# Griffin block of a two-layer decoder trunk: three input-projection turns change their stationary operand, and one gate-input turn is split around the gates

## The reference, cut to what matters

```python
gate, u = jnp.split(x @ w_in, 2, axis=-1)          # w_in: 2048 x 4096
u = causal_depthwise_conv(u, width=4) + conv_b
r = sigmoid(blockwise(u, gate_a_w) + gate_a_b)     # 8 diagonal blocks of 256 x 256
i = sigmoid(blockwise(u, gate_x_w) + gate_x_b)
a = exp(-8 * r * softplus(-lam))
b = u * i * sqrt(1 - a * a)
h = scan(h_t = a_t * h_{t-1} + b_t)                # over positions
y = (gelu(gate) * h) @ w_out
```

## Time and profile before

| what | us |
|---|---|
| median of 3 runs | 2082.54 |
| lowest and highest | 2081.93 to 2082.73 |
| the profiled execution, its own time | 2081.55 |
| its span, first to last instruction | 2079.8 |
| PE busy in it | 2073.0 |
| DVE busy, ACT busy | 1267.6, 969.2 |

### The profile page before, as it was taken

The page is one execution under the profiler, slowest core; times in us unless marked ns, Lnnn a source line. Parts: engine busy times, 40 slices in busy tenths (PEclk is TensorE's granted clock), DMA queues, the critical chain, the costliest instruction groups (busy, mean ns, idle before and its releaser), DMA issues.

```text
span 2079.8 us, 27469 instructions
## 1 busy us (share of the span) xinstructions
PE 2073.0 (100%) x9438; PEld 1724.6 (83%) x9438; DVE 1267.6 (61%) x1247; ACT 969.2 (47%) x1168; POOL 21.3 (1%) x16
## 2 busy tenths in 40 slices
PE   9999999999999999999999999999999999999999
PEld 8888888888888888888888888888888888888887
DVE  6869666665555565555765565775755555555565
ACT  5595555434444443443654444454444434444442
POOL 0000010000000000000100000010000000000000
PEclk9999999999999999999999999999999999999999
DMA  8667758766766766675566667667767766766763
GB/s 259 195 207 243 257 189 264 246 199 206 237 220 185 241 225 200 214 249 173 186 209 206 210 221 233 194 212 243 229 207 221 241 200 201 240 218 224 240 214 120
DMA packets 245884, 451.34 MB, mean 217 GB/s; under 512 B 18720, under 2 KB 49696, under 8 KB 244768
## 3 DMA queue, kind: packets, MB, share of 16 engines
q1 hardware_dynamic: 239888, 440.93, 66.8%
q10 hardware_dynamic: 5904, 9.18, 1.4%
HBM read 421.72 MB, written 20.97 MB: 213 GB/s over the span
## 4 chain that ended last, share of the span: by engine, by line
PE 99%; DMA 0%; DVE 0%; ACT 0%; SPq 0%; issue 0%
PE ps L495 92%; PE ps L486 3%; PE ps L483 1%; PE ps L620 1%; PE ps L589 0%; PE ps L590 0%; PE ps L588 0%; PE ps L658 0%; PE ps L667 0%; DMA f<-in_x_dram 0%; PE ps L668 0%; PE ps L657 0%; PE ps L545 0%; PE ps L681 0%; PE ps L682 0%; DVE f L1335 0%
## 5 line engine op out<-in xcount | busy, mean ns | idle before, releaser
L1083 DVE TENSOR_TENSOR wl<-wst,wh 128x1024 fp32r<-128x1024 f32 x742 | 886.5, 1219 | 380.0 <-ACT wh L781 377.9
L781 ACT ACTIVATE wh<-wst 128x1024 fp32r<-128x1024 f32 x742 | 770.5, 1059 | 690.5 <-PE ps L495 400.6
L495 PE MATMUL ps<-wh,xin 128*128 128x512 f32 x3072 | 824.5, 390 | 0.0
L495 PE MATMUL ps<-wh,hid 128*128 128x512 f32 x2560 | 695.9, 390 | 0.0
L495 PEld LDWEIGHTS ps<-wh,xin 128*128 128x128 f32 x3072 | 575.7, 188 | 118.9
L495 PEld LDWEIGHTS ps<-wh,hid 128*128 128x128 f32 x2560 | 479.5, 188 | 98.9
L495 PE MATMUL ps<-wl,xin 128*128 128x512 f32 x1536 | 472.9, 389 | 0.0
L495 PE MATMUL ps<-wl,hid 128*128 128x512 f32 x1280 | 404.6, 389 | 0.0
L495 PEld LDWEIGHTS ps<-wl,xin 128*128 128x128 f32 x1536 | 288.3, 188 | 60.0
L495 PEld LDWEIGHTS ps<-wl,hid 128*128 128x128 f32 x1280 | 240.2, 188 | 50.0
L1453 DVE STREAM_TRANSPOSE f<-f 128x1024 f32<-128x1024 f32 x32 | 39.9, 1245 | 178.7 <-DMA f<-sq_by_quad 178.7
(11 more groups left out here) (123 smaller groups left out, 563.8 us busy)
## 6 DMA issues: line engine op xcount, KB each, us to landing
wst<-in_mlp_w_dram SPq DMA_DIRECT2D x512, 512.0 KB, 4.7
wst<-in_moba_w_qkv_dram SPq DMA_DIRECT2D x96, 512.0 KB, 4.6
wst<-in_rg_w_in_dram SPq DMA_DIRECT2D x62, 512.0 KB, 4.5
wst<-in_rg_w_out_dram SPq DMA_DIRECT2D x32, 512.0 KB, 5.6
sq_by_quad<-f SPq DMA_DIRECT2D x128, 128.0 KB, 2.6
f<-sq_by_quad SPq DMA_DIRECT2D x32, 512.0 KB, 4.9
wst<-in_moba_w_out_dram SPq DMA_DIRECT2D x32, 512.0 KB, 5.1
f<-in_x_dram SPq DMA_DIRECT2D x8, 256.0 KB, 6.8
```

The source lines that it names most:

```text
L495: return pe.matmul(dst, src[:, c, part, a * P:(a + 1) * P], (wl if low else wh)[:, s, w], start=(c == 0 and part + low == 0), stop=(c == N ...
L781: act.activation(wh[:, off % SPLITS, :], wst[:, slot, :], ACT.Copy).then_inc(wh_done, 1)
L1083: dve.tensor_tensor(wl[:, off % SPLITS, :], wst[:, off % STAGE, :], wh[:, off % SPLITS, :], ALU.subtract).then_inc(wl_done, 1)
```

## The change

The turns 1, 2 and 3 of u take the form with the tokens stationary, as the gate-input turns do. Their results go the same way: copied out by ACT (`take_in`), stored and read back by SP (`store_in`, `read_in`), transposed by DVE (`turn_in`). Turn 0 of u keeps its form. The order of PE becomes: u turns 1 to 3, gate pieces 0 to 3 (groups 0 and 1), blocks 0 to 3 of gate-input turn 0, gate pieces 4 to 7 (groups 2 and 3), blocks 4 to 7 of gate-input turn 0, then gate-input turns 1 to 3. The weight blocks keep running numbers in the new order: 32 to 35 gates, 36 to 39 gate input, 40 to 43 gates, 44 to 47 gate input. The queues of SP, ACT and DVE are written anew for the stretch, the banks of PSUM for the gate pieces are others, and the lists `work` of the gate-input turns start later, since the splits of the first four blocks lie elsewhere.

The diff without what is only renamed (lines are left out where "..." stands):

```diff
...
+U_TOKEN = 3
+HALF = 4
...
         def gate_bank(gb, o):
-            return ps[:, 2 * (gb % 4) + o // 2, (o % 2) * T:(o % 2 + 1) * T]
+            first = 2 * gb if gb < 4 else 2 + 2 * (gb - 4) % 6
+            return ps[:, first + o // 2, (o % 2) * T:(o % 2 + 1) * T]
+        def turn_of(n):
+            return T_U + 1 + n if n < U_TOKEN else T_G + n - U_TOKEN
...
-            with sp.Fori(1, NG) as t:
-                load_turn(w_in, D + t * COLS, B_U + t * BLOCKS)
-            for gb in range(BLOCKS):
+            def store_in(n):
+                sp.wait_ge(psum_free, turn_of(n) + 1)
+                for i in range(GROUP):
+                    sp.dma_start(to_quad[i], in_out[i * 32:(i + 1) * 32, :, :]).then_inc(in_stored, 16)
+            def read_in(n):
+                sp.wait_ge(in_stored, (n + 1) * (16 * GROUP))
+                if n:
+                    sp.wait_ge(in_turned, n)
+                sp.dma_start(in_quad, by_quad.rearrange("p (i n) -> p i n", i=GROUP)).then_inc(in_back, 16)
+            def move_in(n):
+                return {2: lambda: store_in(n), 3: lambda: read_in(n)}
+            def load_gates(gb, b):
                 w, n0 = (rg_gate_a_w, rg_gate_x_w)[gb % 2], gb // 2 * 2
-                sp.wait_ge(wl_done, B_GATES + gb - (STAGE - 1))
+                sp.wait_ge(wl_done, b - (STAGE - 1))
                 sp.dma_start(wst[:, gb % STAGE, :].rearrange("p (k n) -> p k n", n=LRU_W),
...
+            with sp.Fori(1, NG - 1) as t:
+                load_turn(w_in, D + t * COLS, B_U + t * BLOCKS)
+            load_turn(w_in, D + (NG - 1) * COLS, B_U + (NG - 1) * BLOCKS, move_in(0))
+            first = cols_of(w_in, 0)
+            for unit, b in enumerate((B_GATES, B_G)):
+                also = move_in(1 + unit)
+                for k in range(HALF):
+                    if k in also:
+                        also[k]()
+                    load_gates(unit * HALF + k, b + k)
+                for k in range(HALF):
+                    load_block(first[unit * HALF + k], HALF + k, b + HALF + k)
+            load_turn(w_in, COLS, B_G + BLOCKS)
...
             for t in range(2, NG):
-                load_turn(w_in, t * COLS, B_G + t * BLOCKS, move_g(t - 2))
-            also = {**move_g(2), BLOCKS: input_again, **{BLOCKS + n: f for n, f in move_g(3).items()}}
+                load_turn(w_in, t * COLS, B_G + t * BLOCKS, move_in(U_TOKEN + t - 2))
...
@@ -567,18 +577,23 @@
...
-            turn(xin, 1, B_U + BLOCKS, R_X)
-            pair(xin, B_U + 2 * BLOCKS, R_X, T_U + 2)
-            for gb in range(BLOCKS):
-                if gb in (0, 2):
-                    pe.wait_ge(psum_free, T_G + gb // 2 - 1)
-                elif gb >= 4:
-                    pe.wait_ge(sig_done, gb - 3)
+            token_turn(xin, 4, B_U + BLOCKS, R_X)
+            pe.wait_ge(psum_free, T_U + 1)
+            token_turn(xin, 0, B_U + 2 * BLOCKS, R_X)
+            pe.wait_ge(psum_free, T_U + 2)
+            token_turn(xin, 4, B_U + 3 * BLOCKS, R_X)
+            def gate_piece(gb, b):
+                if gb == 0:
+                    pe.wait_ge(psum_free, T_G - 1)
+                elif gb == 2:
+                    pe.wait_ge(psum_free, T_G)
+                elif gb >= HALF:
+                    pe.wait_ge(sig_done, gb - 2)
                 pe.wait_ge(pair_ready, R_CONV + 2 * (gb // 2) + 2)
-                pe.wait_ge(wl_done, B_GATES + gb + 1)
-                s = gb % SPLITS
+                pe.wait_ge(wl_done, b + 1)
+                s = gb % HALF
...
+            for unit, b in enumerate((B_GATES, B_G)):
+                for k in range(HALF):
+                    gate_piece(unit * HALF + k, b + k)
+                if unit == 0:
+                    pe.wait_ge(sig_done, 1)
+                for k in range(HALF):
+                    kb = unit * HALF + k
+                    pe.wait_ge(wl_done, b + HALF + k + 1)
+                    for c in range(kb * KCH, (kb + 1) * KCH):
+                        for part, low in ((0, 0), (1, 0), (0, 1)):
+                            for a in range(HALVES):
+                                mm = token_step(xin, 0, a, c, part, low, HALF + k)
+                    mm.then_inc(mm_done, 1)
+            for t in range(1, NG):
+                if t == 1:
+                    pe.wait_ge(sig_done, 7)
                 pe.wait_ge(psum_free, T_G + t - 1)
                 token_turn(xin, 4 * (t % 2), B_G + t * BLOCKS, R_X)
...
             def conv_start(g):
-                act.wait_ge(psum_free, T_U + g + 1)
+                if 1 <= g <= U_TOKEN:
+                    act.wait_ge(in_turned, g)
+                else:
+                    act.wait_ge(psum_free, T_U + g + 1)
...
-            for t in range(NG):
-                b = B_U + t * BLOCKS
-                if t:
-                    splits(b, t, AHEAD, AHEAD + 1)
-                    conv_start(t - 1)
-                    splits(b, t, AHEAD + 1, AHEAD + CONV)
-                    if t == 1:
...
-                    conv_hi_part(t - 1)
-                splits(b, t, AHEAD + CONV if t else BLOCKS, LATE)
-                take_hl(t % 2, b, u3[:, t * GROUP:(t + 1) * GROUP, :], hl_copied)
-                splits(b, t, LATE)
-            conv_start(NG - 1)
-            for gb in range(BLOCKS):
-                splits(B_GATES, B_GATES // BLOCKS, AHEAD + gb, AHEAD + gb + 1)
-                act.wait_ge(mm_done, B_GATES + gb + 1)
+            def take_in(n, first, b):
+                act.wait_ge(mm_done, b + BLOCKS)
+                if n:
+                    act.wait_ge(in_turned, n)
...
+                    taken = act.activation(by_part, by_col, ACT.Copy)
+                taken.then_inc(psum_free, 1)
...
+            b, no = B_U + BLOCKS, 1
+            splits(b, no, AHEAD, AHEAD + 1)
+            conv_start(0)
+            splits(b, no, AHEAD + 1, AHEAD + CONV)
+            act.wait_ge(sp_abs, 1)
...
+            conv_hi_part(0)
+            splits(b, no, AHEAD + CONV, LATE)
+            take_in(0, 4, b)
+            splits(b, no, LATE)
+            b, no = B_U + 2 * BLOCKS, 2
+            splits(b, no, AHEAD, AHEAD + 6)
+            conv_start(1)
+            splits(b, no, AHEAD + 6, LATE)
+            take_in(1, 0, b)
+            splits(b, no, LATE)
+            b, no = B_U + 3 * BLOCKS, 3
+            splits(b, no, AHEAD, AHEAD + 1)
+            conv_hi_part(1)
+            splits(b, no, AHEAD + 1, AHEAD + 6)
+            conv_start(2)
+            splits(b, no, AHEAD + 6, LATE)
+            take_in(2, 4, b)
+            splits(b, no, LATE)
+            def gate_values(gb, b):
+                act.wait_ge(mm_done, b + 1)
                 dst, bias = ((r3, C_BA), (i3, C_BX))[gb % 2]
                 for o in range(GROUP):
                     c = gb // 2 * GROUP + o
                     sg = act.activation(dst[:, c, :], gate_bank(gb, o), ACT.Sigmoid, bias=prm[:, bias + c:bias + c + 1])
                 sg.then_inc(sig_done, 1)
-                if gb == 1:
-                    conv_hi_part(NG - 1)
+            for k in range(HALF):
+                splits(B_GATES, B_GATES // BLOCKS, AHEAD + k, AHEAD + k + 1)
+                if k == 1:
+                    conv_hi_part(2)
+                gate_values(k, B_GATES + k)
+            splits(B_GATES, B_GATES // BLOCKS, AHEAD + HALF, AHEAD + HALF + 1)
+            conv_start(3)
+            splits(B_GATES, B_GATES // BLOCKS, AHEAD + HALF + 1)
+            conv_hi_part(3)
+            for k in range(HALF):
+                splits(B_G, B_G // BLOCKS, AHEAD + k, AHEAD + k + 1)
+                gate_values(HALF + k, B_G + k)
             act.wait_ge(sp_ready, 1)
             act.wait_ge(sig_done, 8)
...
-                act.wait_ge(g_turned, g + 1)
+                act.wait_ge(in_turned, U_TOKEN + g + 1)
...
-            work = (((1, decay, 0), (2, decay, 1), (2, decay, 2)),
-                    ((1, decay, 3), (2, root, 0), (0, root, 1), (1, root, 2), (1, root, 3)),
+            work = (((1, decay, 0), (1, decay, 1)),
+                    ((0, decay, 2), (1, decay, 3), (2, root, 0), (0, root, 1), (1, root, 2), (1, root, 3)),
                     ((6, gelu, 0), (0, gelu, 1)),
                     ((1, product_hi, 0), (1, product_hi, 1), (4, gelu, 2), (1, product_hi, 2)))
             for t in range(NG):
                 b, no = B_G + t * BLOCKS, B_G // BLOCKS + t
-                off = AHEAD
+                off = AHEAD if t else AHEAD + HALF
...
-                act.wait_ge(mm_done, b + BLOCKS)
-                if t:
...
+                take_in(U_TOKEN + t, 4 * (t % 2), b)
...
-            for t in range(NG):
-                b = B_U + t * BLOCKS
-                if t:
-                    splits(b, AHEAD, AHEAD + 1)
-                    for k in range(1, CONV):
-                        splits(b, AHEAD + k, AHEAD + k + 1)
-                        conv_step(t - 1, k)
-                    splits(b, AHEAD + CONV, AHEAD + CONV + 1)
-                    conv_lo(t - 1)
```

(70 more changed lines are left out.)

55 lines of the change are left out of this document (19 added, 36 removed).

## The result

In alternating runs on one chip the changed kernel took 2085.04 us (median of 16 runs, 2082.61 to 2089.45), the kernel before 2082.07 (16 runs, 2081.61 to 2082.93). That is 2.97 us longer, a ratio of 1.0018 with an interval of 1.0011 to 1.0025. The forecast was 2081.8: the sign is wrong, and the time lies 0.6 us above the range. It is still within the 0.2% that was called no change. The profiled execution of the changed kernel took 2086.9, 1.9 above its median, with a span of 2085.1. So what its trace shows in excess of the span before (2085.1 - 2079.8 = 5.3) is more than the 2.97 of the medians: it is the fourth longest of the 16 executions.

The account below looks back on a forecast made before the run. PE was taken to bound the kernel. The form's -1.29 us and a new wait of 0.55 at gate piece 6 gave -0.74; from the median 2082.54 that made 2081.8 us, range 2080.8 to 2084.4.

Parts of the forecast that it names:

- What bounds the kernel: Whole program: PE bounds, busy 2073.0 of 2079.8 us; other engines' work counts only if PE then waits.
- The form: u turns 1 to 3 with tokens stationary: 65.30 us instead of 66.59, saving 1.29 us, all on the path.
- The estimate of 0.25: u turns 1 to 3: saving in us by the skill's issue-gap rule, which would make the sum +0.3.
- All this I cost at nothing on the path: u turns: added ACT, DVE, SP and DMA work costs PE nothing, except a new wait at gate piece 6.
- the cover of 8 blocks split ahead: u turns: 8 blocks of 2.72 us split ahead cover PE against block loads late by about 6 us.
- The likeness with the gate-input turns: u turns: PE is covered, as the same moves already stand in the gate-input turns, where PE has no wait.
- The wait at piece 6: Gate piece 6: PE waits for conv_lo(3), due 126.73 against 126.19, so 0.54, say 0.55 us.
- The identity activation between sigmoids: Rival, gates: Identity between sigmoids brings one more table load of 1.28 us; net +0.5, 2083.1; chance 0.03.
- the read-back is late: Rival, u turn 3: one slow DMA, wait 0.55 plus 1 to 3.3 us, net +0.3 to +2.6; chance 0.20.
- The test given for it: Piece 6: a wait over 1.5 us, with DVE waiting on the read near 112, would say the DMAs decide.
- the rival of 8 us: Third turned u: read-back very late, both landings 8.0 us, 6.4 more at piece 6, net +5.7, 2088.2; chance 0.07.
- I take the output projection to be covered: Output projection: no cost from the later recurrence, first need being at 208 with four gate-input turns between.

Follow-up runs that it names:

- two kernels, 0.20: Against the changed kernel: u turns neither stored nor read back, 2082.4 us; all seven read-backs issued one block load later, 2081.41 us.
- the control: Kernel before, with only DVE's addition of output-projection turn 0 one split earlier: 2082.1 us against 2081.87, ratio 1.0001.
- the kernel with group 3 in a row: Changed kernel with DVE's three convolution steps of group 3 before the gated input and splits: 2082.61 us; with the addition one split earlier too: 2080.67.
- the form alone: Changed kernel with gate pieces 6 and 7 on group 2's activations and DVE's output-projection addition one split earlier: 2080.52 us, ratio 0.9994.
- with the addition in its place: Changed kernel with gate pieces 6 and 7 on group 2's activations, DVE's addition not moved: 2082.6 us, ratio 1.0007.
- with the wait at piece 6 present: Changed kernel repeated, 2085.38 us, and the changed kernel with DVE's output-projection addition one split earlier, 2083.62 us.
- with group 3's own data: Changed kernel repeated unaltered on the chip of the next three runs: 2085.38 us, ratio 1.0016 to the kernel before.
- the filled one: Changed kernel with 24 matmuls that nothing reads ahead of PE's wait at gate piece 6: 2085.39 us, ratio 1.0019.

## Why the prediction was wrong, step by step

**What bounds the kernel: right.** Every microsecond gained or lost is one of PE's, and the stretch of u turns, gates and gate-input turns holds all but the last wait.

**The form: right.** 65.30 for three turns was worked out; 65.30 is measured in the changed kernel, and 65.30 to 65.34 in the ones that follow. The switches cost nothing that counts: piece 4 starts at 120.93, 22.42 behind the end of turn 3, where 4 x 2.88 + 10.88 = 22.40. The estimate of 0.25 by "TensorE: Matmul & The Clock Gate" of the Trainium skill, section "Back-to-back issue gap", is not borne out: the trace has 1.29.

**"All this I cost at nothing on the path": the step that failed.** The prediction saw that "the block loads behind them are late by about 6 us" and set the cover of 8 blocks split ahead against it. The cover is PE's: PE indeed waited at no weight block. But the same load is also waited for by ACT's split, and ACT's list is in order. Behind that split stand `conv_start(2)` and `take_in(2)`, on which the convolution of group 3 hangs. The price of a held load had to be carried down ACT's list, not only to PE. What was put at nothing was, in the profiled execution, 2.51 us of lateness that PE waited for at piece 6, and 1.54 of clock behind that wait. The sentence "ACT is in order and has no slack behind the end of that turn", from which the chain was started at 98.03, holds where the load isn't held (two kernels, 0.20) and is wrong in the changed one (1.99 and 2.51).

**The likeness with the gate-input turns misled.** "The same moves already stand in the gate-input turns, where PE has no wait" is true, but in the kernel before no step that PE waits for came late by it there.

**The wait at piece 6: the chain's length was right, its start was not.** From its own start the chain needs 28.75 us against the 28.70 listed, and the table above gives a wait of 0.52 to 0.58 on top of the lateness against 0.54. The term was mis-sized by exactly the lateness: 3.03 and 2.53 in place of 0.54. The identity activation between sigmoids brought no table load: `conv_start(3)` (L856) stands at 115.99 with no load before it and none before the sigmoids that follow. Here "ScalarE: Activation LUTs" of the Trainium skill, section "Table sets: the hidden batching unit", by which identity is in every set, agrees with the trace.

**The read-back was in time.** The rival "the read-back is late" came nearest in size (+0.3 to +2.6 net, measured +2.97), by the wrong mechanism: that is luck. Turn 3's transpose at 114.72 went on without a wait for the read issued at 108.93, which landed 4.1 us after its issue, at 113.1. What was late were the loads behind the reads of the turns before. The test given for it, DVE waiting for the read near 112, failed as it should.

**The clock: not priced.** The prediction named it for the rival of 8 us only. The waits of 2.53 and 3.03 us at piece 6 were followed by half clock, which cost 7.34 - 5.76 = 1.6 us and 1.5 us on top of them.

**"I take the output projection to be covered": wrong.** The recurrence was to start some 6 us later. Its table load stands at 140.10 (128.72 before), and its first DVE step (L1305) at 167.56 (155.77 before), so 11.4 and 11.8 later. DVE then works almost without a gap (44.20 of the 45 us from 165 to 210, before 40.52) and comes to the addition at 256.88, 6.9 later than before, where PE is 3.9 later. Before, the addition ended at 251.16 and PE wanted it at 209.42 + 16 x 2.72 = 252.94: there were 1.8 us to spare, and no row of the prediction asked for them. DVE's full list up to 210 is only one part of this lateness. Between 212 and 256 DVE is idle for 17.7 us (before 15.9), always behind a split of ACT's, and ACT in its turn mostly waits for a load. The last such wait stands right ahead of the addition, on ACT and on DVE:

```profile
254.65 1.06 ACT L809 ACTIVATE wh<-wst 128x1024 fp32r<-128x1024 f32 x1 [3.32 <-DMA wst<-in_rg_w_out_dram]
```

```profile
255.74 1.23 DVE L1145 TENSOR_TENSOR wl<-wst,wh 128x1024 fp32r<-128x1024 f32 x1 [3.15 <-ACT wh L809]
```

So here too a load that ACT waits for stands in the path; how the 6.9 us are shared between the late list and the loads stays open. That the addition's place is worth nothing in the kernel before is shown by the control, and that it is worth 1.9 us in the kernel with group 3 in a row by the pair of one set; the 1.8 us in the changed kernel itself agree with that.

**Sum.** By the distances from the kernel before: the form alone -1.53; with the addition in its place +0.42, so the wait there is worth 1.95 (1.76 with the wait at piece 6 present, 2085.38 - 2083.62; 1.94 with group 3 in a row); with group 3's own data +3.20, so the wait at piece 6 with its clock is worth 2.78. The terms of the prediction were -1.29, nothing, and 0.55. These sizes are differences of medians of 10 to 16 runs, some of which overlap; the order of the terms is safer than their tenths.

## What to carry to other kernels

When a transfer is moved into a queue, carry its delay to every engine that waits for the load behind it and down that engine's whole list, not only to the engine that bounds the kernel: eight blocks of cover for PE were no cover for ACT. Where work is put off, price the first thing that the bounding engine needs at the far end of the delayed engine's list, with its margin in us. And price a wait with the clock that it may cost as well (here 1.5 us behind waits of 2.53 and 3.03), then look again at what binds once it is filled: here filling it won nothing, since what the clock gave back went into the next wait.

## What was not expected of the hardware

PE went to half clock, 1.2 GHz, behind waits of 2.29, 2.53 and 3.03 us and stayed at 2.4 GHz behind waits of 0.78, 1.67, 1.70 and 1.79 us and behind the filled one. Each time it had streamed matmuls without a break up to the wait, and the half clock lasted 3.4 us. Half clock showed at a granted 0.50 and a distance of 0.21 us between matmuls of 256 columns instead of 0.12. "TensorE: Matmul & The Clock Gate" of the Trainium skill, section "What's actually happening", has an idle PE fall to 1.2 GHz, as these rows show it.

A 512 KB block load that left right behind a read-back of the same size (0.39 us after it) was waited for until 5.2 us after its issue, and an earlier one, issued at 68.05 behind the read at 67.66, until 74.40, 6.35 us after it. The median of the input projection's loads of that size is 4.5 on the page. Whether the read takes from their share of the DMAs was not tried by itself.
